# Moving the weight blocks of a matmul-bound encoder kernel to other 64-byte pieces of on-chip memory

## What is computed

```python
x += 0.5 * post(SwiGLU(pre(x)))            # FFN 1, hidden width 2816
P  = pre(x) @ w_in                         # 24 column blocks of 128
x += post(concat(norm(neighbourhood_attn), norm(hyena), norm(dilated_attn)) @ w_out)
x += post(cross_attn(pre(x), norm(mem)))   # 4 heads of 256, memory of 256 rows
x += 0.5 * post(SwiGLU(pre(x)))            # FFN 2
```

## The kernel before

| tensor | before, piece | distance from the activations |
|---|---|---|
| `raw0`, `raw1` | 2 | 1 |
| `wh0` to `wh3`, `wl0` to `wl3` | 2 | 1 |
| `tmp`, `side` | 2 | 1 |
| `eye` | 4 | 3 |
| `uH`, `uL`, `hs`, `T1H` to `T4L`, `memH`, `memL`, `qXh`, `kXh` and all others of the big region | 1 | 0 |

## Time and profile before

### The profile page before, as it was taken

How to read it: one execution, slowest core, us unless ns; L and a number is a source line. 1 busy time by engine, 2 the same in 40 slices (tenths; PEclk the granted TensorE clock), 3 DMA queues, 4 the chain that set the end, 5 groups by cost and what they waited for, 6 DMA issues and landing times.

```text
span 2325.6 us, 38259 instructions
## 1 busy us (share of the span) xinstructions
PE 2295.1 (99%) x15046; PEld 2056.9 (88%) x15046; DVE 1577.4 (68%) x2191; ACT 1064.5 (46%) x1765; POOL 109.3 (5%) x185
## 2 busy tenths in 40 slices
PE   7999999999999999999999999999999999999998
PEld 7999888777888899998899998887778888999987
DVE  7999437645365499994399993476464654999833
ACT  5445335227454364443364443352284544644522
POOL 0000000610000000000000000007000000000000
PEclk9999999999999999999999999999999999999999
DMA  4333323240234133323233333232402341333332
GB/s 140 110 113 123 117 82 136 73 142 25 73 110 145 55 110 109 108 99 109 82 111 108 108 102 110 79 136 73 147 19 73 118 145 46 113 115 108 117 92 81
DMA packets 66225, 236.00 MB, mean 101 GB/s; under 512 B 8882, under 2 KB 10632, under 8 KB 65600
## 3 DMA queue, kind: packets, MB, share of 16 engines
q1 hardware_dynamic: 57600, 209.74, 27.1%
q0 software_dynamic: 8224, 24.12, 3.2%
q10 hardware_dynamic: 288, 0.59, 0.1%
HBM read 232.29 MB, written 2.12 MB: 101 GB/s over the span
## 4 chain that ended last, share of the span: by engine, by line
PE 95%; ACT 2%; DVE 2%; issue 1%; DMA 1%; DVEq 0%; SPq 0%; ACTq 0%
PE bank L399 14%; PE bank L403 14%; PE bank L401 14%; PE bank L506 11%; PE bank L504 11%; PE bank L505 11%; PE bank L653 4%; PE bank L456 2%; PE bank L458 2%; PE bank L457 2%; PE bank L628 2%; PE bank L724 1%; PE bank L441 1%; PE bank L613 1%; PE bank L589 1%
## 5 line engine op out<-in xcount | busy, mean ns | idle before, releaser
L313 DVE TENSOR_TENSOR wl<-raw,wh 128x1024 fp32r<-128x1024 f32 x232 | 301.9, 1301 | 371.9 <-ACT wh L308 371.2
L308 ACT ACTIVATE wh<-raw 128x1024 fp32r<-128x1024 f32 x232 | 245.0, 1056 | 492.5 <-PE bank L403 412.1
L399 PE MATMUL bank<-wh,hs 128*128 128x512 f32 x704 | 278.5, 396 | 0.0
L403 PE MATMUL bank<-wh,hs 128*128 128x512 f32 x704 | 276.1, 392 | 0.0
L401 PE MATMUL bank<-wl,hs 128*128 128x512 f32 x704 | 273.6, 389 | 0.0
L504 PE MATMUL bank<-uH,wh 128*128 128x256 f32 x960 | 268.0, 279 | 0.0
L506 PE MATMUL bank<-uH,wl 128*128 128x256 f32 x960 | 267.8, 279 | 0.0
L505 PE MATMUL bank<-uL,wh 128*128 128x256 f32 x960 | 267.8, 279 | 0.0
L1367 DVE TENSOR_TENSOR wl<-S,wh 128x1024 fp32r<-128x1024 f32 x160 | 194.5, 1216 | 0.0
L506 PEld LDWEIGHTS bank<-uH,wl 128*128 128x128 f32 x960 | 181.3, 189 | 0.0
L505 PEld LDWEIGHTS bank<-uL,wh 128*128 128x128 f32 x960 | 181.3, 189 | 0.0
(11 more groups left out here) (273 smaller groups left out, 5866.3 us busy)
## 6 DMA issues: line engine op xcount, KB each, us to landing
raw<-in_w_proj SPq DMA_DIRECT2D x128, 512.0 KB, 3.5
raw<-in_w_first SPq DMA_DIRECT2D x96, 512.0 KB, 3.6
raw<-in_w_second SPq DMA_DIRECT2D x88, 512.0 KB, 3.4
side<-in_w_first SPq DMA_DIRECT2D x40, 512.0 KB, 3.5
raw_value<-in_w_first SPq DMA_DIRECT2D x40, 512.0 KB, 4.2
gain_rows<-in_grow POOLq DMA_DIRECT2D x15, 512.0 KB, 5.2
strip<-bias_of_distance POOLq DMA_DIRECT2D x2, 2688.0 KB, 13.7
strip<-in_rpb POOLq DMA_DIRECT2D x96, 24.0 KB, 2.2
```

The source lines that it names most:

```text
L308: e.activation(wh[u % RING][:], raw[u % RAWS][:], ACT.Copy).then_inc(high_ready, 1)
L313: e.tensor_tensor(wl[u % RING][:], raw[u % RAWS][:], wh[u % RING][:].bitcast(F32), ALU.subtract).then_inc(split_ready, 1)
L399: e.matmul(b[:, c], still_h, hi[:, c], start=first and c.start == 0, stop=False)
L403: mm = e.matmul(b[:, c], still_l, hi[:, c], start=False, stop=last and c.stop == n)
```

## The change

Small tensors are moved, and the ring's blocks are padded apart. The four blocks of the ring now begin 0, 4, 5 and 6 pieces after the activations (modulo 8 pieces). `negmax` (256 bytes) stands between `wh0` and `wh1`, `stat` (now padded to 128 bytes) between `wh3` and `wl0`, and `den` (256 bytes) between `wl0` and `wl1`; blocks 1 and 2 are 64 bytes longer than what is used of them. `ALIGN` goes from 106 to 48.

```diff
-ALIGN = 106
+
+PIECE = 16
+ALIGN = 48
...
-        wh = [sb(f"wh{i}", [P, D], F32R) for i in range(RING)]
-        wl = [sb(f"wl{i}", [P, D], F32R) for i in range(RING)]
+        behind = (0, PIECE, PIECE, 0)
+        wh = [sb("wh0", [P, D], F32R)]
+        negmax = sb("negmax", [P, ITEMS])
+        wh += [sb(f"wh{i}", [P, D + behind[i]], F32R)[:, 0:D] for i in range(1, RING)]
+        stat = sb("stat", [P, 6 * NT + 8])[:, 0:6 * NT].rearrange("p (a i) -> p a i", a=6)
+        wl = [sb("wl0", [P, D], F32R)]
+        den = sb("den", [P, ITEMS])
+        wl += [sb(f"wl{i}", [P, D + behind[i]], F32R)[:, 0:D] for i in range(1, RING)]
...
-        stat = sb("stat", [P, 6, NT])
...
-        negmax = sb("negmax", [P, ITEMS])
-        den = sb("den", [P, ITEMS])
```

## The result

| kernel | median us | range | executions |
|---|---|---|---|
| before | 2315.42 | 2312.68 to 2318.16 | 2 |
| after | 2353.74 | 2353.51 to 2353.98 | 2 |

The ratio is 1.0155, with a 95% interval of 1.0116 to 1.0194. The forecast was 2310, its range 2263 to 2350: wrong in sign, and 3.7 us outside the range. The profiled executions differ by 26.6 us of span (2352.2 against 2325.6), the medians by 38.3. Both numbers need an explanation.

What follows compares the result with a forecast made beforehand. The prediction took TensorE, busy 99% of the span, as the bound, so matmul spacing sets the time. Its terms, 10.1 + 3.4 - 15.6 - 3.8 = -5.9 us on the median 2315.4, gave 2310 us, range 2263 to 2350.

Steps and rivals of the forecast that it cites:

- The bound: Whole kernel: TensorE, busy 99% of the span, sets the time through the spacing of its matmuls.
- Block 0 with 256 columns, +10.1: 2400 matmuls of block 0, going from distance 1 to 0: spacing from 115.8 to 120 ns, +10.1 us.
- The two levels at 512 columns: 512-column matmuls: 228.9 and 233.3 ns taken as a low and a high level, 4.4 ns apart.
- Block 0 with 512 columns, +3.4: Block 0 at distance 0: 233.3 ns assumed, 288 weight-stationary matmuls unchanged, 768 weight-moving ones 4.4 ns dearer, +3.4 us.
- Blocks 1 to 3 with 256 columns, -15.6: 6240 matmuls at distances 4, 5, 6: always the lower level, 113.3 for 115.8 ns, -15.6 us.
- Blocks 1 to 3 with 512 columns, -3.8 and 0: 864 weight-stationary matmuls go from 233.3 to 228.9 ns, -3.8 us; weight-moving ones stay at 228.9, 0.
- The step to the median, -12.0 us: Final sum: -5.9 us, worked out on the profiled 2327.44 whole, was applied to the median, 12.0 lower, 2315.4.
- VectorE, `eye` and the small tensors at 0: Low parts on VectorE, transposes reading `eye`, and moved small tensors: no time change, with +3 us kept for the range.
- The cap of 112.1 ns: FFN loops: VectorE, busy 178.14 of 180 us, keeps matmul spacing from going under 112.1 ns.
- Every distance but 1 is like 0: Rival, all blocks: loads cross the stream twice per matmul everywhere, 2365 or 2393 us; chance 0.10.
- It does nothing: Rival, whole kernel: the loss's cause lies in TensorE itself and addresses do not matter, 2315 us; chance 0.08.
- Levels are drawn anew: Rival, all matmuls: spacing levels fall by chance, -27 to +31 us, 2289 to 2346; high end over 2330, chance 0.10.

Runs made afterwards that it cites:

- 1, 5, 5, 5: Changed kernel's layout, but with the four weight blocks at these distances in pieces from the activations; 2326.76 us, ratio 1.0028 to the kernel before.
- the shifted kernel: Changed kernel with ALIGN 32 for 48, all activations 64 bytes lower, blocks at distances 1, 5, 6, 7; 2342.5 us, ratio 1.0086 to the kernel before.

## Why the prediction was wrong

**What the runs showed in its place.** Spacing in ns by (stationary minus moving) in pieces, modulo 4, from the kernels with one distance for all. With 512 columns both roles were run, and the signed difference decides, not which operand moves; with 256 columns the weights were always stationary:

| residue | 256 columns | 512 columns |
|---|---|---|
| 0 | 120.0 | 226.7 |
| 1 | 113.3 or 117.8 | 233.3 |
| 2 | 118.8 | 232.4 |
| 3 | 117.7 | 229.0 |

One group stands outside the table: the 192 matmuls of the memory's values (weights moving, residue 3 at distance 1) ran at 233.4 in both layers in the kernels with the small tensors alone, with distance 5, with 1, 5, 5, 5 and with `hs` moved, and at 233.3 in one layer and 228.9 in the other in the kernel before.

**The bound: right.** TensorE is 99% busy in both kernels, and the time went with the spacing and nothing else.

**Block 0 with 256 columns, +10.1: right.** It measured +9.7, and 119.8 where 120 came from the earlier trace rows. A single row of another part of the program was enough to price 2400 matmuls.

**The two levels at 512 columns: a misreading, but for one group.** The prediction took 228.9 and 233.3 as a low and a high level. Outside the memory's values they are two residues, 3 with weights moving and 1 with weights stationary; in every profile at distance 1 each part of the kernel has 228.9 to 229.2 with weights moving and 233.2 to 233.3 with weights stationary (`hs`, where it was moved, apart). So the 864 stationary ones had no lower level to go to at their residue.

**Block 0 with 512 columns, +3.4: wrong in sign.** 288 stationary ones went from 233.3 to 227.5, -1.6 us; 768 moving ones stayed, 0.0. The bounds, 228.9 to 240, did not even hold 227.5, since both assumed that a distance bad for 256 columns is bad for 512.

**Blocks 1 to 3 with 256 columns, -15.6: the step that failed.** It measured 8.1 + 4.6 + 6.1 = +18.8, which is 34.4 us off. The step said that "the place where they meet goes to the middle of the load". It took the 512-byte load as the circle on which distance counts. The circle is 256 bytes: 4 pieces are 0, the place the prediction itself had priced at 120 for block 0. Nothing in the trace of before fixed the period, and of the three distances only 5 is a good one. Block 2, at distance 5, should then have stayed at 115.6 and came out at 117.6: in the changed kernel it is nearly always the upper level of its residue. In the shifted kernel, where two blocks of four have residue 1, those blocks came out at 115.8 and 116.1. That a loop with neighbours off residue 1 draws the upper level more often fits both, but is argued, not shown.

**Blocks 1 to 3 with 512 columns, -3.8 and 0: small misses.** Stationary ones gave -1.6 + 0.1 - 0.2 = -1.7, moving ones -1.6 + 0.8 + 2.7 = +1.9; the table says which go where (block 1 is residue 0 in both roles, block 3 residue 2 in both, block 2 residue 1 standing and 3 moving). Block 0 moving, 229.2, is the exception: some 450 of its 768 spacings are 224 to 228 as they should be, some 260 are 231 to 236. The dear ones come just after block 3: the first six after it average 231.7, the later ones of the same stretch 226.7 to 228.0. What is carried over is not known.

**The step to the median, -12.0 us: wrong, and worth a quarter of the miss.** The sum was taken from the profiled execution's 2327.4 and carried over to the median of 2315.4 as if the 12 us were noise. They were loops: the profiled execution had two at the upper level; of the two timed ones, 2318.16 lies in the cluster of one, and 2312.68 nearest to that of none. The changed kernel shows no such steps, its loops all run at 119 and its two executions lie 0.5 us apart, so the difference belongs on the profiled execution: 2327.4 + 26.6 = 2354.0. (That 2353.7 was measured is no test of this, as the profiled execution of the changed kernel, 2353.98, is one of the two.) Of the miss of 43.7 us, the terms account for 32.5 (26.6 against -5.9) and this step for 12.0; rounding 2309.5 up (0.5) and the 0.3 between 2354.0 and 2353.7 go the other way.

**VectorE, `eye` and the small tensors at 0: right.** 1216 and 1220 ns again, transposes at 110, and the kernel with the small tensors alone at 1.001. (`eye` is read by 802 transposes, not some 720.) The cap of 112.1 ns was never reached.

**The rivals.** "Every distance but 1 is like 0" is what happened in the loops, which run at 119; with 512 columns the opposite held at 0, and so the 2365 to 2393 were not reached. "It does nothing" fell: the same instructions at other addresses run at 113 to 120 ns. By the Trainium skill's rule of two independent ports ("SBUF — State Buffer", "Who interferes with whom") the time would have been unchanged; these runs disagree, by up to 1.8% of the kernel's time (distance 2). "Levels are drawn anew" was real, but it moves the kernel before, not the changed one; its sum for all high is 8640 x 1.9 + 3072 x 4.4 = +29.9, not +31, and its 512-column terms rest on the misread levels.

**What stays open.** Why float32r loses 7 to 13 ns at 256 columns and 13 to 20 at 512 at all; why the two shapes rank the residues in another order; what makes the period 256 bytes, and the half pieces dear; what picks the level after a pause, and why some layouts come out at the upper one more often.

## What to carry to other kernels

Where TensorE is the bound and spaces its matmuls wider than its columns need, the start addresses of the two operands are a variable to be measured: shift one of them through 32-byte steps over 256 bytes, with one number, and read the spacing per shape and role before padding blocks apart. Compute a spacing from all start times, not from record lengths, and look at the executions one by one: a kernel with two levels has its times in steps, so a profile and a median may stand on different steps. When the rows of a trace give one point of a periodic function (here 0 and 1), the other points have no bounds from it, and both signs deserve their weight.

## What the hardware showed that was not expected

- Spacing of float32r matmuls depends on the operands' address difference with a period of 256 bytes, 113.3 to 120.0 ns at 256 columns and 226.7 to 233.3 at 512, and of the whole pieces the best for one shape (1) is the worst for the other.
- The same matmuls at the same addresses can run at two levels: 113.3 and 117.8 at distance 1, 117.3 and 118.6 at 1.5. A pause of 50 ns can come with a switch, and the level then holds to the end of a loop, some 190 us, so executions at distance 1 differ by steps of 7 to 8 us.
- 32 bytes matter too: at 0.5 and 1.5 pieces all 512-column matmuls cost 233 to 234 ns and the kernel 2356 to 2361 us.
